# Two-block transformer on one core: token rows of the first experts through device memory, a ring of eight places, layer 1's modulation with layer 0

## What is computed

```python
for l in range(DEPTH):                      # DEPTH = 2
    mod   = silu(c)     @ w_mod[l] + b_mod[l]      # w_mod[l]: 1024 x 6144
    mod_c = silu(c_ctx) @ w_mod[l] + b_mod[l]
    sh1, sc1, gt1, sh2, sc2, gt2 = split(mod, 6)
    h = rms_norm(x, norm_mix[l]) * (1 + sc1) + sh1
    x = x + gt1 * mixer(h)                  # attention; layer 0: mixer_ab, layer 1: mixer_c
    tokens = rms_norm(x, norm_ffn[l]) * (1 + sc2) + sh2     # layer 0: 512 rows, layer 1: 256
    x = x + gt2 * hier_moe(tokens)          # 32 experts, each token goes to 2 of them
# an expert: (silu(xb @ w1[e]) * (xb @ w3[e])) @ w2[e];  w1, w3: 1024 x 512, w2: 512 x 1024
```

## Time and profile before

| | us |
|---|---|
| median of 3 runs | 2726.3 (2717.1 to 2728.8) |
| the profiled execution | 2726.1, its span 2724.3 |
| PE busy | 2472.1 (91%) |
| DVE busy | 862.3 (32%) |
| ACT busy | 398.1 (15%) |
| DMA | 587.8 MB, mean 216 GB/s |

### The profile page before, as it was taken

One profiled execution on the slowest core, in us unless ns is written; L12 is line 12 of the kernel. 1 busy time (PEld: TensorE's weight loads), 2 busy tenths in 40 slices (PEclk: granted clock), 3 DMA queues, 4 the chain that ended last, 5 costly groups with the idle time before them and its releaser, 6 DMA issues.

```text
span 2724.3 us, 29734 instructions
## 1 busy us (share of the span) xinstructions
PE 2472.1 (91%) x11286; PEld 1362.8 (50%) x11286; DVE 862.3 (32%) x1704; ACT 398.1 (15%) x964; POOL 78.7 (3%) x104
## 2 busy tenths in 40 slices
PE   5989889999999988998799999998889999879998
PEld 3456464454445444444534443334558744476853
DVE  2666232232323235625322222224451102371001
ACT  1035020000000001023100000101321000140000
POOL 0200000000000001200000000000000000000000
PEclk8999989999999999999899999998899999989999
DMA  7521128888888885211499999992303443503441
GB/s 279 185 93 63 62 86 356 338 361 348 339 342 357 358 320 175 72 62 35 163 405 393 414 412 388 402 394 85 114 31 124 164 151 99 173 1 103 150 164 69
DMA packets 143282, 587.82 MB, mean 216 GB/s; under 512 B 9185, under 2 KB 19425, under 8 KB 93921
## 3 DMA queue, kind: packets, MB, share of 16 engines
q1 hardware_dynamic: 142768, 584.55, 56.1%
q10 hardware_dynamic: 288, 1.19, 0.1%
q0 software_dynamic: 144, 0.97, 0.1%
HBM read 585.63 MB, written 1.05 MB: 215 GB/s over the span
## 4 chain that ended last, share of the span: by engine, by line
PE 75%; DMA 9%; DVE 9%; issue 3%; ACT 2%; POOL 1%; SPq 1%; DVEq 0%; ACTq 0%; POOLq 0%
PE psum L2108 13%; PE psum L1763 10%; DMA ring<-in_w 8%; PE psum L2304 8%; PE psum L2317 8%; PE psum L2094 7%; PE psum L2121 7%; PE psum L2171 5%; PE psum L1696 3%; PE psum L2222 3%; PE psum L1755 2%; PE psum L1702 1%; POOL rstd L372 1%; PE psum L1710 1%; PE psum L2262 1%
## 5 line engine op out<-in xcount | busy, mean ns | idle before, releaser
L2108 PE MATMUL psum<-ring,arena 128*64 128x512 f32 x2048 | 464.8, 601 | 44.0 <-DMA ring<-in_w 41.7
L1763 PE MATMUL psum<-ring,hT 128*128 128x512 f32 x832 | 362.4, 593 | 5.4 <-issue 2.1
L2108 PEld LDWEIGHTS psum<-ring,arena 128*64 128x64 f32 x2048 | 149.8, 138 | 351.7 <-issue 322.0
L1763 PEld LDWEIGHTS psum<-ring,hT 128*128 128x128 f32 x832 | 155.9, 190 | 195.3 <-issue 191.1
L1394 DVE TENSOR_TENSOR arena<-arena,psum 128x512 f32<-128x512 f32 x204 | 140.5, 689 | 336.7 <-PE psum L2121 336.7
L2171 PE MATMUL psum<-ring,arena 128*64 128x512 f32 x1024 | 226.8, 595 | 0.0
L2317 PE MATMUL psum<-ring,arena 128*128 128x512 f32 x512 | 220.3, 592 | 3.2 <-DVE arena L1595 3.2
L2304 PE MATMUL psum<-hT,ring 128*128 128x256 f32 x1024 | 221.5, 379 | 1.3 <-DVE hT L1460 1.3
L2094 PE MATMUL psum<-arena 128*128 128x128 f32 x1632 | 200.7, 281 | 9.1 <-DVE arena L1382 9.1
L2304 PEld LDWEIGHTS psum<-hT,ring 128*128 128x128 f32 x1024 | 194.4, 190 | 28.0 <-DVE hT L1460 1.7
L2094 PEld LDWEIGHTS psum<-arena 128*128 128x128 f32 x1632 | 191.8, 196 | 28.8 <-issue 28.8
(11 more groups left out here) (269 smaller groups left out, 1939.6 us busy)
## 6 DMA issues: line engine op xcount, KB each, us to landing
ring<-in_w SPq DMA_DIRECT2D x384, 1024.0 KB, 8.5
ring<-in_w_ff SPq DMA_DIRECT2D x64, 1024.0 KB, 5.4
ring<-in_w_mod SPq DMA_DIRECT2D x32, 1024.0 KB, 7.7
hT<-in_w_mod SPq DMA_DIRECT2D x16, 1024.0 KB, 10.3
ring<-in_w_in_c SPq DMA_DIRECT2D x12, 1024.0 KB, 5.9
ring<-in_w_in SPq DMA_DIRECT2D x12, 1024.0 KB, 6.4
ring<-in_w_out SPq DMA_DIRECT2D x8, 1024.0 KB, 5.2
ring<-in_w_in_ab SPq DMA_DIRECT2D x6, 1024.0 KB, 5.2
```

The lines of the kernel that those rows point to most:

```text
L1763: inst = pe.matmul(bank, hT[:, k, P * m:P * m + P], w[k], start=k == 0, stop=k == KB - 1)
L2108: inst = pe.matmul(out[64 * e:64 * e + 64, :], xgT[:, b, k, 64 * e:64 * e + 64], m, start=k == 0, stop=k == KB - 1)
```

## The change

- `x_rows` is a new tensor in device memory, 64 rows for each of 32 experts and 128 spill rows. ACT fills it with zeros from `blank` at the start of `attention_ab`. In `moe(0)` DVE works out for each token its two rows (`places`), and POOL writes hrow there with eight indirect transfers (`dispatch`). SP waits for them after the first eight chunks, and loads each pair's 128 rows (0.5 MB) in the same queue as the weights, into `x_slots` (in hT). PE turns them with eight transposes (`turn_rows`) instead of the gather; the first pair is gathered as before. Layer 1 keeps the gather.
- In both expert loops the ring has eight places; the two more are `rows`. SP waits for the squares (ss_ready) before it fills them.
- w_mod[1] is computed with layer 0: blocks 0 to 5 in `heads`, behind those of w_mod[0], blocks 6 to 11 after `attention_ab`. Its product leaves the expert loop and the place behind it. modT is kept for each layer.

```diff
+    def resize(self, size):
+        self.size, self.at = size, 0
+    def take(self):
+        slot = self.at % self.size
+        before = self.user.get(slot)
+        self.user[slot] = self.count
+        self.at += 1
+        self.count += 1
+        return slot, before
...
+        modT = [sb(f"modT{l}", [P, 48, 2]) for l in range(DEPTH)]
+        x_rows = nc.dram_tensor("x_rows", (EXPERTS * SLOTS + P, D), f32).ap()
+        slot_base, spill, x_place = sb("slot_base", [P, EXPERTS]), sb("spill", [P, 1]), sb("x_place", [P, 8])
+        x_index = sb("x_index", [P, 8], i32)
...
-        mrow = arena[:, 9216:10240].rearrange("p (b n) -> p b n", b=2)
+        mrow = arena[:, 9216:11264].rearrange("p (b n) -> p b n", b=4)
+        blank = arena[:, 17408:18432]
...
+        x_slots = [hT[:, 2 * b:2 * b + 2, :].rearrange("p a n -> p (a n)") for b in range(2)]
+        def slot_at(i):
+            return ring[:, i, :] if i < RING else rows[:, 2 * (i - RING):2 * (i - RING) + 2, :].rearrange("p a n -> p (a n)")
...
+            def dispatch():
+                pool.wait_ge(x_zeroed, 16)
+                pool.wait_ge(x_placed, 1)
+                for m in range(4):
+                    for j in range(2):
+                        at = bass.IndirectOffsetOnAxis(ap=x_index[:, 2 * m + j:2 * m + j + 1], axis=0)
+                        pool.indirect_dma_start(x_rows, at, hrow[:, m, :], None).then_inc(x_scattered, 16)
...
             rsqrt_rows(4)
+            dispatch()
             pads()
...
+                act.wait_ge(blanked, 1)
+                act.dma_start(x_rows.rearrange("(a p) n -> p a n", p=P),
+                              blank[:, None, :].to_broadcast([P, EXPERTS * SLOTS // P + 1, D])).then_inc(x_zeroed, 16)
                 exps(0)
                 exps(1)
...
             def mod_rest():
                 scalers(4)
-                for c in range(PAIRS // 2, MOD_BLOCKS, 2):
-                    mod_rows(c)
-                    mod_columns(1, c)
                 mod_gains(1, 0)
                 mod_gains(1, 1)
                 gate_diagonals(1)
...
                     if tile == 0 and c:
                         mod_columns(0, 2 + 2 * c)
+                        mod_columns(1, 2 * c - 2)
                     if tile == 3:
                         mod_rows(4 + 2 * c)
+                        mod_rows(2 * c, 2)
                 mod_columns(0, 8)
+                mod_columns(1, 4)
                 mod_gains(0, 1)
...
+                def places():
+                    def tab(a, w=EXPERTS, at=0):
+                        return route[:, a, 0:nt, at:at + w]
+                    dve.tensor_tensor(tab(5), tab(13), slot_base[:, None, :].to_broadcast([P, nt, EXPERTS]), ALU.add)
+                    dve.tensor_scalar(tab(7), tab(13), float(SLOTS), float(2 * SLOTS * EXPERTS), ALU.is_ge, ALU.mult).then_inc(v_step, 1)
+                    dve.wait_ge(v_step, so_far(v_step))
+                    dve.tensor_tensor(tab(5), tab(5), tab(7), ALU.add).then_inc(v_step, 1)
+                    dve.wait_ge(v_step, so_far(v_step))
+                    for j in range(2):
+                        dve.tensor_tensor(tab(6), tab(8 + j), tab(5), ALU.mult).then_inc(v_step, 1)
+                        dve.wait_ge(v_step, so_far(v_step))
+                        dve.tensor_reduce(x_place[:, j:8:2], tab(6), AX, ALU.add).then_inc(v_step, 1)
+                        dve.wait_ge(v_step, so_far(v_step))
+                    dve.tensor_tensor(x_place[:, :], x_place[:, :], spill[:, 0:1].to_broadcast([P, 8]), ALU.min).then_inc(v_step, 1)
+                    dve.wait_ge(v_step, so_far(v_step))
+                    dve.tensor_copy(x_index[:, :], x_place[:, :]).then_inc(x_placed, 1)
+                if l == 0:
+                    selector(pick[:, 0], 0, False, True)
+                    places()
+                    selector(share[:, 0], 0, True, True)
+                else:
...
+                    selector(pick[:, 1], 2, False, True)
...
-                        selector(share[:, 1 - b], 4 * i + 2 * b + 2, True, False)
-                        selector(pick[:, b], 4 * i + 2 * b + 4, False, True)
+                        selector(share[:, 1 - b], 4 * i + 2 * b + 2, True, l == 0)
+                        if l:
+                            selector(pick[:, b], 4 * i + 2 * b + 4, False, True)
...
             mod_rows(10)
+            mod_rows(6, 2)
             mod_columns(0, 10)
+            mod_columns(1, 6)
+            dve.wait_ge(x_zeroed, 16)
             gate_diagonals(0)
+            for c in (8, 10):
+                mod_rows(c)
+                mod_columns(1, c)
             add_output(0, [0, 1, 2, 3])
             moe(0)
             mod_rest()
...
                 for x in (c, c + 1):
                     pe.wait_ge(mod_row, mixed.next())
                     pe.wait_ge(v_free, v_done.value(back=3))
                     bank = v_bank()
-                    folded(bank, mrow[:, x % 2, :]).then_inc(mm_v, 1)
+                    folded(bank, mrow[:, at + x % 2, :]).then_inc(mm_v, 1)
...
                         waiting.append((c, tile))
                         if modulate and c and tile == tiles[0]:
                             mod_folds(2 + 2 * c)
+                            mod_folds(2 * c - 2, 2)
                     if modulate:
                         mod_products(4 + 2 * c)
+                        mod_products(2 * c)
                 turn(*waiting.pop())
                 if modulate:
                     mod_folds(8)
+                    mod_folds(4, 2)
...
+                def turn_rows(b):
+                    pe.wait_ge(x_fetched[b], fetched[b].next())
+                    for h in range(2):
+                        for k in range(4):
+                            kk = 4 * h + k
+                            inst = transpose(psum[:, 5 + h, P * k:P * k + P], x_slots[b][:, P * kk:P * kk + P])
+                        inst.then_inc(mm_a, 1)
+                        a_done.n += 1
...
-                tallies.update({c: 24 // RING for c in chunk_in})
+                tallies.update({c: 24 // EXPERT_RING for c in chunk_in})
+                slots.resize(EXPERT_RING)
                 if l == 0:
-                    tallies.update({mod_in: 2, mod_out: 2})
+                    tallies.update({f: 1 for f in fetched})
...
                     for b in range(2):
                         pe.wait_ge(a_free, a_done.value())
                         up(psum[:, 4, :], b)
                         add_pair()
-                        if l == 0 and b == 1:
-                            pe.wait_ge(mod_loaded, mod_in.next(2))
-                            mod_block(psum[:, 7, :], [mod_w[k // 4][:, k % 4, :] for k in range(KB)], mod_product)
-                            mod_out.n += 1
                         pe.wait_ge(v_free, v_done.value(back=3))
                         bank = v_bank()
                         up(bank, b)
-                        if l == 0 and b == 1:
-                            pe.wait_ge(mod_taken, mod_out.value())
-                            folded(psum[:, 7, :], mod_sums).then_inc(mod_product, 1)
-                            mod_out.n += 1
                         pe.wait_ge(pick_ready, picks.next())
-                        gather(1 - b, 0)
+                        if l == 0:
+                            turn_rows(1 - b)
+                        else:
+                            gather(1 - b, 0)
                         pe.wait_ge(v_free, v_done.value())
                         bank = v_bank()
                         for f in range(4):
                             inst = transpose(bank[:, P * f:P * f + P], act_[:, P * f:P * f + P])
                         inst.then_inc(mm_v, 1)
-                        gather(1 - b, 1)
+                        if l:
+                            gather(1 - b, 1)
                         bank = v_bank()
                         for m in range(nt):
                             inst = transpose(bank[:, P * m:P * m + P], share[:, b, m, :])
+                            if l == 0 and m == 0:
+                                inst.then_inc(x_turned, 1)
                         inst.then_inc(mm_v, 1)
                         pe.wait_ge(v_free, v_done.value(back=1))
...
             mod_products(10)
+            mod_products(6)
             mod_folds(10)
+            mod_folds(6, 2)
+            for c in (8, 10):
+                mod_products(c)
+                mod_folds(c)
             output(all4, 0, gates_of=0)
             moe(0)
-            for c in range(PAIRS // 2, MOD_BLOCKS, 2):
-                mod_products(c)
-                mod_folds(c)
             norm(4)
...
-                slot = count[0] % RING
-                if count[0] >= RING:
-                    freed.n = count[0] - RING + 1
+                slot, before = slots.take()
+                if before is not None:
+                    freed.n = before + 1
                     sp.wait_ge(used, freed.value())
```

(71 more changed lines are left out.)

69 lines of the change are left out of this document (30 added, 39 removed).

## The result

| | before | after |
|---|---|---|
| median in the same series, us | 2721.7 (4 runs) | 2652.4 (4 runs) |
| the profiled execution, its span | 2726.1, 2724.3 | 2647.3, 2645.5 |
| PE busy | 2472.1 (91%) | 2396.6 (91%) |
| DMA | 587.8 MB, mean 216 GB/s | 609.3 MB, mean 230 GB/s |

What follows compares the result with a forecast made beforehand. The prediction took PE as the bound, with DMA following behind. Its terms, -111 - 11 + 24 + 26 + 6 + 3 - 5 = -68, took the median of 2726.3 to 2658 us, range 2622 to 2702.

Steps and rivals of the forecast that it cites:

- Part 1: First experts: loaded rows replace the gather, DMA becomes the bound at 401 GB/s; minus 111 including the loop's start.
- Rival E: First experts: tokens land late, SP's look-ahead is lost, each pair keeps a 5.2 us chunk wait; 2741 us, chance 0.03.
- D: Rival: the first experts' 340 GB/s stay, since their idle 15% is not the ring's; 2748 us, chance 0.03.
- Part 2: Start of the first experts' loop: eight scatters take 10.5 plus 3.5 us, SP is free at 392.
- Rival C: Start of the loop: eight scatters of 10.7 us each, SP free at 463, DMA 71 us late; 2729 us, chance 0.07.
- Part 3: Layer 1's modulation moved: the four blocks after the first experts' loop leave the path, minus 11; costs arise at the front.
- (b): After attention_ab: PE waits for mod chunks landing slot by slot, so output comes later; plus 26 us.
- (a): Between blocks of heads_ab: w_mod[1] chunks stand ahead of the next weights, and folds are added; plus 24 us.
- (c): Front, between the heads and after attention: PE's gaps lower its clock, so products run slower; plus 6 us (0 to 15).
- Part 4: Zero fill of 8.9 MB issued by ACT before exps(0): ACT may be held; plus 3 us.
- rival B: Front costs more: ACT held 14, lower clock 15, both w_mod stretches 10 more; 2688 us, chance 0.20.
- Part 5: Eight places in the second experts: only the two chunks loaded ahead count; minus 5 us (0 to 13).

Runs made afterwards that it cites:

- half_up8: The changed kernel with half of each up projection's products left out in both layers, every chunk still transferred: 2631.9 us, one run.
- thin8: The changed kernel with eight places from the start until attention_ab and only 128 of 512 columns of w_mod[1]'s blocks 0 to 5 transferred: 2632.7 us, one run.
- ring6: The changed kernel with six places instead of eight in both expert loops: 2714.4 us, 0.9948 of before.
- mod_behind: The changed kernel with all 12 blocks of layer 1's modulation placed behind the first experts: 2627.3 us, 0.9624 of before.
- heads8: The changed kernel with eight places from the start until attention_ab: 2635.4 us, 0.9656 of before.
- gather_ring8: The changed kernel with the gather back in layer 0, no zero fill, scatters or row loads; eight places and moved modulation kept: 2733.0 us, 1.0013 of before.

## Why the prediction was right, and where not

**Part 1, the first experts: right about PE's chain, low in rate.** -122 instead of -111. PE's chain of 31.2 us a pair is 31.15. The forecast had the transfers as the bound, by 1 to 1.5 us a pair over this chain; they are level with it (31.1), and PE waits for no chunk. half_up8 shows that they would be next. The sign of 32 to 33 us a pair didn't come. The step that failed is "I take 401, since it contains the hiccups": 421 was measured. 201 MB take 502 us at 401 and 477 at 422, 25 us less. From SP's release to the last landing it was 483, and the release came 2 us later behind the gather than told, so the last chunk landed 17 us earlier than forecast. PE ended 9.3 us behind that landing instead of 3, since its own chain now was as long, and 11 us reached the time. (The loop before ended at 1008.8 and not at the sum's 1008.0, which is within this reading.)

The wait for x_turned cost nothing, as said: no chunk is waited for in the loop. Rival E falls, and D with it: 420 GB/s instead of the 340 that D kept.

The forecast weighed only one of the Trainium skill's figures, 358 GB/s. That was half of a reading: by the Trainium skill (HBM Reference, "Specifications (TRN2)") this is a core's share while its neighbour streams too, and a core alone measures about 425. The trace agrees with the second, 420 to 421 GB/s in the two loops. Set beside the 401 of the earlier trace rows, that page's 425 gives an estimate of 6% that this stage had left to gain; the runs gave 5%.

**Part 2, the start: right.** 15.5 us for the scatters against 14, SP free 18.7 us after the gather began against 16.6. Rival C (10.7 us each) falls: they are issued 1.3 us apart, all eight had landed 6.4 us after the last was issued, so they overlap. By the Trainium skill (DMA: Bandwidth & Descriptors, "Anatomy of one DMA") the forecast had an estimate of 25.6 for eight one after another; by this trace they aren't one after another, and the whole took 15.5.

**Part 3, behind the loop: right** (-10.5 against -11). **(b) behind the attention: right**, 28.3 against 26. **(a) between the heads: wrong by half**, 48 against 24 and a share of the clock's 6. In the forecast's own steps, for the first border: tile 0 was to start 8.0 later and started 10.1 later, which is near. Behind it only the doubled folds, 1.8, were to come, and 9.6 came: 1.7 and 3.0 on the tiles, 2.8 on the folds, 1.9 of waiting for DVE's columns, which had no term, and 0.2 of rest. The clock, (c), was sized at 6 for the whole front; at this border alone the tiles (4.7), the folds beyond their doubled work (1.0) and the last products (3.5 for 16 that take 1.9 at full clock) are 7.3. thin8 shows the same from the other side: with the waits for chunks at the first border down from 5.6 to 2.1 us, 30 of the 48 us remained.

**The 5.6 us in layer 1's attention** aren't the change's. The stretch from the norm to the second gather does the same work in all runs. It took 280.4 us before, 281 to 283 in ring6, half_up8, mod_behind and heads8, and 285 to 286 in after and the other five. What decides between the two levels isn't shown.

**Part 4, the fill: right** in being small (1.2 against 3). ACT was not held: 0.42 us for the issue, so rival B's item of a held ACT did not occur. Its lower clock did, and of its two longer stretches the one between the heads.

**Part 5, the second experts: wrong**, -26.7 against -5. The step that failed is "DMA is 99% busy, so only the two chunks loaded ahead count". A busy share of 0.99 at 401 GB/s was no ceiling: a share of 1.01 stands beside 421 after, and ring6 has 0.99 beside 404 again. The missing gain stood in the trace of before as 25.7 us of PE's waits for chunks, 16 of them, one for each pair. The forecast counted the stage as bound by the transfers and gave these waits no term; ring6 and gather_ring8 (473.9 with eight places and nothing else changed there) show that they were the ring's. The upper end of the term, 13, was too low as well.

## What to carry to other kernels

A DMA share near 1 doesn't say that the rate is the ceiling. Look for regular short waits of the reader for its chunks, multiply rate by landing time for what is under way, and if that is well under the ring's size, the release of places is the limit: more places, or an earlier release, give the rest. Work moved into a stretch "where DMA had slack" still costs its instructions there, and here the dense tiles beside it ran 1.7 and 3.0 us longer at a lower clock; put it where PE stands idle anyway. A total that comes out right can hide two errors of opposite sign, so a forecast is judged by its stages.

## What the runs showed of the hardware

- With about 4.2 to 6.1 MB under way one core loaded 415 to 421 GB/s for hundreds of us. With about 3.3 MB it was 386 in the first experts of ring6, at a DMA share of 0.95, and with 3.4 MB 404 in its second, at a share of 0.99.
- Eight indirect transfers of 0.5 MB each were issued 1.3 us apart by POOL and had all landed 15.5 us after the first began.
- 8.9 MB of zeros were issued in 0.42 us of ACT's queue and landed in 32.0 us, 279 GB/s. Weight chunks shared the DMA engines for most of it (383 GB/s in all), so this is not what a lone fill takes.
- In thin8 the granted clock went from 1.00 to 0.50 within a run of 32 products of 2 columns, and the next tile of 16 products took 10.0 us instead of 7.0 to 7.1.
